# Norms with tile 0 ahead of tile 1's sum, step sizes with tokens moving, and new places in the mixer's orders

## The reference

```python
for l in range(DEPTH):          # 2
    x = _layernorm(DEEPNORM_ALPHA * x + FFN_RES * _swiglu(x, ffn1_w_in[l], ffn1_w_out[l]), ln1_g[l], ln1_b[l])
    mix = _hybrid_mixer(x, l, ...)   # A: attention, B: state-space scan, C: stick-breaking
    x = _layernorm(DEEPNORM_ALPHA * x + mix, ln2_g[l], ln2_b[l])
    x = _layernorm(DEEPNORM_ALPHA * x + FFN_RES * _swiglu(x, ffn2_w_in[l], ffn2_w_out[l]), ln3_g[l], ln3_b[l])
```

## Time and profile before

| | us |
|---|---|
| median of 3 runs (2444.74 to 2447.61) | 2444.77 |
| the profiled execution | 2445.78 |
| its span, first to last instruction | 2443.8 |

### The profile page before, as it was taken

How to read it: one execution, slowest core, us unless ns; L and a number is a source line. 1 busy time by engine, 2 the same in 40 slices (tenths; PEclk the granted TensorE clock), 3 DMA queues, 4 the chain that set the end, 5 groups by cost and what they waited for, 6 DMA issues and landing times.

```text
span 2443.8 us, 33499 instructions
## 1 busy us (share of the span) xinstructions
PE 2261.6 (93%) x12480; PEld 1916.5 (78%) x12480; DVE 1654.8 (68%) x2142; ACT 1154.2 (47%) x1658; POOL 353.5 (14%) x143
## 2 busy tenths in 40 slices
PE   8998999989989989989999999899798847999999
PEld 6886888778868868878988778688687846887877
DVE  5775676588667757765765777677666454667997
ACT  4443454554444434444554644444353023546875
POOL 3431000000024414501000000244101000000000
PEclk9998999899999999999999999999989757999999
DMA  9765543344557657746443436577441001758996
GB/s 304 239 214 148 176 146 117 110 138 135 192 186 233 219 166 232 236 139 202 147 131 104 130 120 198 149 252 236 152 120 38 2 1 34 230 190 277 360 360 225
DMA packets 320170, 426.86 MB, mean 175 GB/s; under 512 B 28193, under 2 KB 220081, under 8 KB 320033
## 3 DMA queue, kind: packets, MB, share of 16 engines
q1 hardware_dynamic: 315904, 412.45, 53.1%
q0 software_dynamic: 4016, 12.56, 1.8%
q10 hardware_dynamic: 112, 0.04, 0.0%
HBM read 423.90 MB, written 1.05 MB: 174 GB/s over the span
## 4 chain that ended last, share of the span: by engine, by line
PE 82%; DVE 6%; issue 5%; ACT 2%; DVEq 2%; DMA 1%; POOL 1%; PEld 0%; POOLq 0%; PEldq 0%; SPq 0%; ACTq 0%
PE ps L267 19%; PE ps L269 19%; PE ps L268 19%; PE ps L514 10%; PE ps L3187 4%; PE ps L300 2%; DVE lo L254 1%; ACT hi L250 1%; PE ps L1056 1%; DVE room L1141 1%; PE ps L505 1%; PE ps L899 1%; DVEq L733 1%; DVE room L1340 1%; PE ps L1249 0%
## 5 line engine op out<-in xcount | busy, mean ns | idle before, releaser
L254 DVE TENSOR_TENSOR lo<-raw,hi 128x1024 fp32r<-128x1024 f32 x737 | 1015.6, 1394 | 490.6 <-ACT hi L250 484.0
L250 ACT CAST hi<-raw 128x1024 fp32r<-128x1024 f32 x737 | 767.5, 1048 | 672.3 <-PE ps L269 500.7
L267 PE MATMUL ps<-hi,xT_hi 128*128 128x512 f32 (+2 forms) x1440 | 572.8, 398 | 5.6 <-issue 4.9
L269 PE MATMUL ps<-hi,xT_lo 128*128 128x512 f32 (+2 forms) x1440 | 560.6, 389 | 0.0
L268 PE MATMUL ps<-lo,xT_hi 128*128 128x512 f32 (+2 forms) x1440 | 560.2, 389 | 0.0
L267 PEld LDWEIGHTS ps<-hi,xT_hi 128*128 128x128 f32 x1440 | 278.4, 193 | 58.1 <-issue 6.5
L269 PEld LDWEIGHTS ps<-hi,xT_lo 128*128 128x128 f32 x1440 | 277.4, 193 | 56.7
L268 PEld LDWEIGHTS ps<-lo,xT_hi 128*128 128x128 f32 x1440 | 278.3, 193 | 51.0
L684 POOL TENSOR_SCALAR room<-room,vecs 128x1536 f32<-128x1536 f32 x28 | 134.3, 4797 | 234.7 <-DMA room<-in_w_ada 234.7
L267 PE MATMUL ps<-xT_hi,hi 128*128 128x256 f32 x544 | 159.8, 294 | 0.0
L268 PE MATMUL ps<-xT_lo,hi 128*128 128x256 f32 x544 | 154.5, 284 | 0.0
(11 more groups left out here) (531 smaller groups left out, 3210.3 us busy)
## 6 DMA issues: line engine op xcount, KB each, us to landing
raw<-in_w_mix_in SPq DMA_DIRECT2D x368, 256.0 KB, 2.9
raw<-in_ffn_w_in SPq DMA_DIRECT2D x352, 256.0 KB, 3.5
raw<-in_ffn_w_out SPq DMA_DIRECT2D x176, 256.0 KB, 2.9
raw<-in_w_gate SPq DMA_DIRECT2D x128, 256.0 KB, 4.7
raw<-in_w_up SPq DMA_DIRECT2D x128, 256.0 KB, 6.2
raw<-in_w_down SPq DMA_DIRECT2D x128, 256.0 KB, 5.2
room<-in_w_ada SPq DMA_DIRECT2D x32, 768.0 KB, 6.3
raw<-in_w_branch SPq DMA_DIRECT2D x96, 256.0 KB, 3.1
```

The source lines that it names most:

```text
L250: nc.scalar.copy(hi[c.hi_slot][:, 0:c.cols], raw[c.slot][:, 0:c.cols]).then_inc(rounded, 1)
L254: nc.vector.tensor_tensor(lo[c.slot][:, 0:c.cols], raw[c.slot][:, 0:c.cols], hi[c.hi_slot][:, 0:c.cols], ALU.subtract).then_inc(split, 1)
L267: pe.matmul(out, a[0], b[0], start=start, stop=False)
L269: return pe.matmul(out, a[1], b[0], start=False, stop=stop)
```

## The change

In the norms the ticks of the last chunks (two of a feed-forward part, four of the mixer's output product) are moved from ahead of the norm to behind it, as `act_tail` and `dve_tail`. Tile 0 is added on its own; behind `OutProduct` it is also centered before tile 1 is added, elsewhere after tile 1's centering and after the power is asked for. The step sizes become a block of kind `few`: the 16 weight columns are stationary and the 256 tokens move, the result [16, 256] is copied by ACT, transposed by PE and copied by DVE. In the mixer `dve_scale` goes in two parts to h = 7 and 8, the decay steps move by two to four, the first taps to h = 42, 44 and 46, `dve_cum` ahead of the taps of h = 51, `act_exp` of quads 0 and 1 one half on, the gating of A's second half into h = 73 ahead of `dve_weights`, and the first turn of C from h = 1 to 2. In the second block the window, the output product, the modulation and the experts are one phase; the output product's first chunk is rounded and split ahead of the window's last turn, and it finishes tile 0 before tile 1, as `OutProduct` does, with tile 0's gated add and square following at once.

```diff
@@ -372,7 +372,11 @@
                 pe.wait_ge(split, ch.n + 1)
-            if self.kind == "tok":
+            if self.kind == "few":
+                w = ch.parts(self.ks, self.n)
+                for k in range(half * KT // 2, (half + 1) * KT // 2):
+                    ins = three(pe, ps[0:self.n, self.banks[0], 0:TOK], [v[:, k, :] for v in w], [s[:, k, :] for s in self.stat], k == 0, k == KT - 1)
+            elif self.kind == "tok":
                 w = ch.parts(self.ks, self.n)
@@ -578,7 +582,10 @@
             self.pairs_of_units(act, unit)
-            ticks(self.Dn[-1], None)
+
+        def act_tail(self, act):
+            for c in self.Dn[-1]:
+                tick_act(act, c)
         def dve(self, dve):
@@ -719,30 +729,38 @@
             pool.dma_start(ln_par[:, 1, :], self.b[self.l:self.l + 1, :].partition_broadcast(P)).then_inc(norm_par, 16)
+        def add(self, dve, t):
+            self.source.await_sum(dve, t)
+            acc = ps[:, 2 * t:2 * t + 2, :].rearrange("p a b -> p (a b)")
+            return nc.vector.scalar_tensor_tensor(out=x[:, t, :], in0=acc, scalar=self.r, in1=x[:, t, :], op0=ALU.mult, op1=ALU.add)
+
+        def center_first(self, dve):
+            dve.wait_ge(ln_mean, self.number + 1)
+            nc.vector.scalar_tensor_tensor(out=merged[:, 0, :], in0=x[:, 0, :], scalar=small[:, 28:29], in1=ln_par[:, 0, :], op0=ALU.add, op1=ALU.mult)
+
         def dve(self, dve):
...
             st, mv = view(small, 0, 2, 6), small[:, 24:26]
+            early = isinstance(self.source, OutProduct)
             dve.wait_ge(ln_scaled, n)
-            for t in range(TT):
-                self.source.await_sum(dve, t)
-                acc = ps[:, 2 * t:2 * t + 2, :].rearrange("p a b -> p (a b)")
-                ins = V.scalar_tensor_tensor(out=x[:, t, :], in0=acc, scalar=self.r, in1=x[:, t, :], op0=ALU.mult, op1=ALU.add)
-                if t == 0:
-                    ins.then_inc(ln_added, 1)
+            self.add(dve, 0).then_inc(ln_added, 1)
+            dve.wait_ge(norm_par, n * 32)
+            if early:
+                self.center_first(dve)
+            self.add(dve, 1)
             dve.drain()
...
             V.bn_aggr(mv, st.rearrange("p a b -> p (a b)"))
-            dve.wait_ge(norm_par, n * 32)
-            dve.wait_ge(ln_mean, n)
-            V.scalar_tensor_tensor(out=y[:, 0, :], in0=x[:, 0, :], scalar=small[:, 28:29], in1=ln_par[:, 0, :], op0=ALU.add, op1=ALU.mult)
             dve.drain()
...
             V.scalar_tensor_tensor(out=y[:, 1, :], in0=x[:, 1, :], scalar=mv[:, 0:1], in1=ln_par[:, 0, :], op0=ALU.subtract, op1=ALU.mult)
+            if not early:
+                self.center_first(dve)
             dve.drain()
@@ -756,6 +774,7 @@
                 self.gap.dve(dve)
+            self.source.dve_tail(dve)
         def pool(self, pool):
@@ -776,6 +795,7 @@
             nc.scalar.activation(spare, x[:, 0, :], ACT.Square, bias=small[:, 28:29], accum_out=small[:, 29:30]).then_inc(ln_squared, 1)
+            self.source.act_tail(act)
             if self.toT is not None:
@@ -1012,14 +1032,15 @@
             nc.vector.tensor_scalar(self.st[:, 16:32], self.squares, 1.0 / P, LN_EPS, ALU.mult, ALU.add).then_inc(pow_asked, 1)
-        def dve_scale(self, dve):
+        def dve_scale(self, dve, part):
             dve.wait_ge(pow_done, self.power)
-            for h in range(HA):
+            for h in range(part * HA // 2, (part + 1) * HA // 2):
                 for t in range(TT):
...
                                                          op0=ALU.mult, op1=ALU.mult)
-            ins.then_inc(self.ready, 1)
+            if part:
+                ins.then_inc(self.ready, 1)
     class StickBreaking:
@@ -1206,6 +1228,20 @@
         def pool(self, pool):
...
             nc.gpsimd.tensor_tensor(self.st[:, 8:12], self.st[:, 4:8], const("minus_half")[:, 0:4], ALU.pow).then_inc(pow_done, 1)
+
+        def turn_steps(self, pe, b):
+            pe.wait_ge(evac_act, b.evac_act)
+            for t in range(TT):
+                ins = pe.transpose(ps[:, b.banks[1], t * HB:(t + 1) * HB], self.dtT[:, t * P:(t + 1) * P], ident[0:HB, 0:HB])
+            ins.then_inc(self.dt_turned, 1)
+
+        def act_steps(self, act, b):
+            act.wait_ge(used, b.done)
+            nc.scalar.copy(self.dtT, ps[0:HB, b.banks[0], 0:TOK]).then_inc(evac_act, 1)
+
+        def dve_steps(self, dve, b):
+            dve.wait_ge(self.dt_turned, self.l + 1)
+            nc.vector.tensor_copy(dt_raw, ps[:, b.banks[1], 0:TT * HB].rearrange("p (t h) -> p t h", t=TT)).then_inc(evac_dve, 1)
         def turn_taps(self, pe, bank):
@@ -1389,6 +1425,14 @@
             self.done = self.chunks[-1].used
+
+        def act_tail(self, act):
+            for c in self.chunks[4:]:
+                tick_act(act, c)
+
+        def dve_tail(self, dve):
@@ -1515,7 +1559,9 @@
                     stick.outputs(pe, j)
-                if h == 50:
+                if h == 27:
+                    scan.turn_steps(pe, self.dt)
+                elif h == 50:
                     pe.wait_ge(stick.copied, stick.nth(6))
@@ -1535,7 +1581,7 @@
                 b.pe(pe, c, h % 2)
-                if h == 1:
+                if h == 2:
                     pe.wait_ge(stick.copied, stick.nth(7))
@@ -1613,7 +1659,10 @@
                             act.wait_ge(diff.out_done, diff.nth(HA - 1))
-                        b.evacuate_act(act)
+                        if b is self.dt:
+                            scan.act_steps(act, b)
+                        else:
+                            b.evacuate_act(act)
                 if h == 1:
@@ -1635,14 +1684,14 @@
                     stick.act_out(act, j)
-                if h == 29:
+                if h == 32:
                     scan.act_decay(act)
-                elif 42 <= h < 45:
+                elif h in (42, 44, 46):
                     if h == 42:
...
                         act.wait_ge(stick.scored, stick.nth(7))
-                    scan.convolve.act_first(h - 42)
+                    scan.convolve.act_first((h - 42) // 2)
                 elif h == 49:
@@ -1652,10 +1701,8 @@
                     scan.act_xs(act, h - 55)
-                elif h == 71:
+                elif h == 72:
                     scan.act_exp(act, 0)
-                elif h == 73:
-                    scan.act_exp(act, 1)
                 if h % 2 and h > 1:
@@ -1665,7 +1712,9 @@
                     gates_of_last(b, c)
-                if h == 2:
+                if h == 0:
+                    scan.act_exp(act, 1)
+                elif h == 3:
                     self.turns_c[0].act(act)
@@ -1690,7 +1739,7 @@
             self.out.second.act(act)
-            for ch in self.out.chunks[2:]:
+            for ch in self.out.chunks[2:4]:
                 tick_act(act, ch)
         def dve(self, dve):
@@ -1733,14 +1782,14 @@
                             self.A.dve_bias(dve, self.A.gate.index(b))
-                        else:
+                        elif b is not self.dt:
                             if b is self.xbc[0]:
...
                     diff.dve_moments(dve)
-                elif h == 6:
-                    diff.dve_scale(dve)
+                elif h in (7, 8):
+                    diff.dve_scale(dve, h - 7)
                 elif h == 12:
@@ -1754,18 +1803,19 @@
                     stick.dve_stay(dve, j)
-                if h == 27:
-                    dve.wait_ge(evac_act, self.dt.evac_act)
+                if h == 29:
+                    scan.dve_steps(dve, self.dt)
+                elif h == 30:
                     dve.drain()
                     scan.dve_decay(dve)
-                elif h == 30:
+                elif h == 34:
                     scan.dve_table(dve)
-                elif 44 <= h < 53:
+                if h == 51:
+                    scan.dve_cum(dve, 1)
+                if 44 <= h < 53:
                     if h == 44:
...
                     scan.convolve.dve(dve, (h - 44) // 3, 1 + (h - 44) % 3)
-                if h == 51:
-                    scan.dve_cum(dve, 1)
                 elif h in (56, 57):
@@ -1778,11 +1828,11 @@
                 elif h == 73:
+                    self.A.dve(dve, 1)
                     scan.dve_weights(dve, 0)
...
                     tick_dve(dve, b.chunks[c])
-            self.A.dve(dve, 1)
             fourth = self.grid(self.fourth)
@@ -1795,7 +1845,7 @@
                     scan.dve_weights(dve, 1)
-                elif h == 2:
+                elif h == 3:
                     self.turns_c[0].dve(dve)
@@ -2033,16 +2083,16 @@
         def add_gated(self, dve, gate):
...
                 acc = ps[:, 2 * t:2 * t + 2, :].rearrange("p a b -> p (a b)")
+                out_2.await_sum(dve, t)
                 nc.vector.tensor_tensor(merged[:, t, :], gates2[:, gate, :], acc, ALU.mult)
-            dve.drain()
-            nc.vector.tensor_tensor(x[:], x[:], merged[:], ALU.add)
+                dve.drain()
```

(60 more changed lines are left out.)

41 lines of the change are left out of this document (14 added, 27 removed).

## The result

The changed kernel took 2363.21 us (median of 4 runs, 2359.15 to 2364.53), the kernel before 2444.76 (4 runs, 2439.1 to 2447.61). The ratio is 0.9666, with a 95% interval of 0.9645 to 0.9687: 82 us faster, and the forecast of 2369.0 is 6 us above it. The profiled execution of the changed kernel took 2364.53 us, its span 2362.5, the mean granted clock 0.964 (before 0.944).

The account below looks back on a forecast made before the run. TensorE, busy for 93% of the span, was taken as the bound; norms 24.2, two mixer layers 43.5 and second block 9.1 sum to 76.8 us off 2445.8, giving 2369.0. Range 2360 to 2380, chance 0.64.

Parts of the forecast that it names:

- the first sums: Mixer's stick-breaking sums: logits ahead of branch A's scaling cut PE's wait from 3.3 to 1.6; with clock 4.0 per layer.
- the turn: Branch C's first turn in the mixer: PE's 5.0 us wait for A's gating goes; with clock 7.35 us per layer.
- the second block: Output product's first split 3.4 us sooner, clock 2.1, gated add and squares at the end 3.8 off; together 9.1 us.
- The step sizes: Mixer's step-size products: 24 of 256 moving columns replace 48 of 16, clock stays up; net 6.9 us off per layer.
- The clock: PE's low clock behind waits and old step-size products comes back with shorter gaps; 14.4 us of the sum.
- (b) and the copy: Mixer's last sums: spread taps and earlier cumulative copy yield 3.5 us per layer; DVE is the chain, copy wait stays 1.3.
- The norms: Six norms: ticks behind, tile 0 added early; 3.95 each in three feed-forward, 4.6 in two mixer, 3.1 last; 24.2 us.
- The clock does not come back: Rival: shortened gaps still lower PE's clock after waits and norms; 28 us less gain, 2397 us; chance 0.14.
- DVE's order becomes the bound: Rival: waits counted as gone return one instruction later; 15 us less, 2384, 5 more if mixer-norm splits are late; chance 0.14.
- Slower: Rival: 16 stationary columns count as little work, low clock spreads into following products; slower than before from 167 us; chance 0.02.

Follow-up runs that it names:

- second_alone: Kernel before with only the second block's part: one phase from the window on, output product in two token halves, first chunk ready early; 2432.96 us.
- no_cum: Changed kernel with the cumulative copy put back behind the taps of h = 51; 2371.7 us.
- tails_alone: Kernel before with only the last chunks' ticks moved behind the norm, the norm's own order as before; 2422.6 us.
- steps_alone: Kernel before with only the step sizes' part: 16 weight columns stationary, 256 tokens moving, result transposed, decay steps later; 2429.48 us.
- scale_alone: Kernel before with only the scaling of branch A's heads split in two parts behind the first logits; 2434.79 us.
- steps_halves: Changed kernel with the step sizes' 24 products of 256 moving columns made as 48 of 128; 2367.0 us.

## Why the prediction was right, and where it was not

**The waits: right one by one.** By my sum 51.6 us of waits were to go: 24.2 in the norms, 3.4 at the first sums, 7.0 at the last sums and the copy, 10.0 at the turn, 7.0 in the second block. The same ones fell by 20.5 and 3.6 (the last norm, 14.57 to 10.96), 3.7, 3.9 + 2.0, 10.0 and 6.7: 50.4. PE's idle time as a whole fell by 43.3 only, since in this execution x landed 2.1 us later (wait of 6.7 to 8.8), the wait in the window's last stretch grew by 2.0, where PE, at the higher clock, comes earlier to the same DVE work, and a wait of 1.7 that was not there before came up in the second block; the other 1.3 is spread over small ones.

**The step sizes: right.** 24 products 0.113 us apart, 2.8 us after 8.6, with the clock at 1.00; no visible wait at the two transposes. My 0.12 came from blocks that load 128 columns, and those of 16 are a little closer together. The estimate of 0.109 each, by the gap formula of the Trainium skill (TensorE: Matmul & The Clock Gate, Back-to-back issue gap), lies 0.004 under what was measured. The row with a stationary side of 16 that was missing is now there: its load takes 0.09 us, one of 128 columns just before it 0.19.

**The clock: right in kind, too small.** I had 14.4 us coming back from it. PE's busy time fell by 38.0, of which the step sizes' products are 2 x 5.8 = 11.6, so 26.4 came from the clock. The step that fell short is the list of places: I priced the clock at seven places (three in each layer, one in the second block), and left every other stretch as it was in the trace of before. Cut at the same waits of PE, the two traces say where it was short. Between the first and the last sums the busy time fell by 9.3 in each layer, where my terms give 9.2 (5.7 - 0.3 + 1.5 + 2.3). From the last sums to the mixer's norm it fell by 3.6, where I had 2.35. In the second block, from 1838.75 of the kernel before on, it fell by 12.7, where I had 2.1: the window's last stretch alone gave 5.7 (15.03 to 9.33) and 3.7 of span with nothing edited in it. As second_alone shows that form without an edit ahead of it, this part of the surplus is not shown to be the change's doing. Missing waits of 8 and surplus clock of 12 nearly cancel; that the total came within 6 us owes something to this, which is luck.

**(b) and the copy: the reasoning failed, with a small loss.** I said that the copy's wait would stay at 1.3 and that only what the copy moves, 3.5, counts. But PE starts from the stay's end, and the copy came 1.73 nearer to it, more than the whole wait of 1.25. It went to 0.24 per layer, 2.0 off in both, and not to nothing, because PE came sooner too: with the copy in its old place no_cum has 2.01. "DVE is the chain" was true of its list and not of PE's wait for one row in it.

**The norms: the sum right, the shares not.** The prediction gave 2.2 us to the ticks and 1.17 to the adding order. In tails_alone the ticks bring both. That I counted no clock behind the norms was right: from the end of the norm's wait to PE's next wait of 2 us or so (the first sums', or that for the last hidden tile) its busy time is the same in both kernels within 0.3 us, five times over (before and after: 175.5 and 175.4, 183.5 and 183.3, 183.2 and 183.3, 175.5 and 175.8, 183.5 and 183.6).

**The rivals.** *The clock does not come back* fell in steps_alone and, by the count over all traces, in scale_alone: behind the gap of 3.3 us the clock was down in 11 of 18 places, behind that of 1.4 in none of 10. Behind the norms, where waits of 7.9 and 10.5 became 4.1 and 5.9, nothing came back, as this rival had it. My reading that waits of 2.3 us leave the clock up was drawn from one of four: at 198.81 of the same trace it was down for 3.4 us behind such a wait. *DVE's order becomes the bound* fell: the splits behind the norms made no wait. *Slower*: 16 stationary columns don't lower the clock, in 2.9 us of them (changed kernel) or in 3.1 (steps_halves).

**What is left.** The old form still stands once in the changed kernel: a block of 16 columns in the second block's projections, 48 products with 16 moving columns, over which PE is busy throughout and the clock is down:

```profile
1747.90:1756.10 8.20, 8.20 (x51) 8.20 (x50) 3.57 (x7) 3.25 (x7) 0.00 (x0) 0.64 0.27 89
```

The same swap may pay there too; no run tried it.

## What to carry to other kernels

An engine's queue in order hides the cheapest gains: ask of each item just ahead of a critical step whether it is needed there, and whether what it waits for comes later than what the step waits for; two to four ticks moved behind a norm gave, in time, as much as the whole reordering. Price each wait from the two things PE stands between, the last release and the next one, and not from how full the releasing engine is. And a kernel with many short gaps has a clock that shifts in places far from the edit, and between executions of the same work: for effects under some 5 us take neither the total as proof nor one trace of each kernel, and look in several traces at the stretch that the edit touches.

## What the runs showed of the hardware

- A product with 16 stationary and 128 moving columns starts 0.060 us after the one before it; with 256 moving 0.113 (steps_halves and the changed kernel). The loads of 16 columns, 0.09 us each in the trace, overlap and bound nothing.
- The granted clock fell to half under 48 products with 16 moving columns while PE was busy throughout (0.53 over 11 us; in all 18 places in the mixers), and stayed at 1.00 under products with 16 stationary ones (in all 10).
- A wait of 3.3 us had the clock down behind it in 11 of 18 places, the same wait cut to 1.4 us in none of 10.
- The same kernel runs at different times with its mean clock: the 23 runs of the kernel before range from 2437.75 us (clock 0.949) to 2448.07 (0.945). The Trainium skill (TensorE: Matmul & The Clock Gate, What's actually happening) has the gate's time base run free of the kernel, which agrees; no run here shows that time base itself.
